# Hybrid encoder step: the output projection's and the FFN's first operands are loaded and split inside the stage in front of them, and the first norm's rows and weights come first in the DMA queue

## The reference

```python
def _layer(l, x, ...):
    z = _rms(x, w["norm1_g"]) @ w["w_in"]          # first norm and input projection
    ...                                            # four mixers: A window, B differential, C latent, M memory
    o = jnp.concatenate([oa, ob, oc, om], axis=-1) # each (B, S, 256)
    x = x + o @ w["w_o"]                           # output projection, 1024 x 1024
    y, new["conv"] = _conv_ffn(_rms(x, w["norm2_g"]), prev, w["f_win"], cw, cb, w["f_wout"])
    return x + y, new

def _conv_ffn(h, prev, w_in, cw, cb, w_out):       # D_FF = 2816
    up = jnp.concatenate([prev.astype(h.dtype), h @ w_in], axis=1)
    ...                                            # causal conv of width 3, c = a | b
    return (jax.nn.silu(a) * b) @ w_out, up[:, S:]
```

## Time and profile before

| | |
|---|---|
| median of 3 runs | 3217.75 us (3211.58 to 3218.52) |
| the profiled execution | 3207.85 us, span of its trace 3205.8 us |
| mean granted TensorE clock | 0.941 of full |
| busy: TensorE, VectorE, ScalarE, GpSimd | 2896.8, 1747.3, 1206.6, 125.9 us |
| DMA engines' share of the span | 15.7% |

### The profile page before, as it was taken

The page is one execution under the profiler, slowest core; times in us unless marked ns, Lnnn a source line. Parts: engine busy times, 40 slices in busy tenths (PEclk is TensorE's granted clock), DMA queues, the critical chain, the costliest instruction groups (busy, mean ns, idle before and its releaser), DMA issues. The chain is left out here.

```text
span 3205.8 us, 49139 instructions
## 1 busy us (share of the span) xinstructions
PE 2896.8 (90%) x19104; PEld 2739.9 (85%) x19104; DVE 1747.3 (55%) x2837; ACT 1206.6 (38%) x2561; POOL 125.9 (4%) x248
## 2 busy tenths in 40 slices
PE   6888879789899999999978888788789999999997
PEld 5686768579899999999957768667789999999997
DVE  3467754643555555555545596465436555545554
ACT  5556644652322222222246574456423222212223
...
DMA packets 182224, 160.89 MB, mean 50 GB/s; under 512 B 14488, under 2 KB 169880, under 8 KB 181528
## 3 DMA queue, kind: packets, MB, share of 16 engines
q1 hardware_dynamic: 182040, 158.45, 15.7%
...
## 5 line engine op out<-in xcount | busy, mean ns | idle before, releaser
L1837 PE MATMUL ps<-h_hi,w_hi 128*128 128x352 f32 x2496 | 546.6, 327 | 43.3 <-DVE w_lo L1948 22.7
L1837 PE MATMUL ps<-h_hi,w_lo 128*128 128x352 f32 x2496 | 540.1, 324 | 0.0
L1837 PE MATMUL ps<-h_lo,w_hi 128*128 128x352 f32 x2496 | 539.9, 324 | 0.0
L1837 PEld LDWEIGHTS ps<-h_hi,w_hi 128*128 128x128 f32 x2496 | 426.8, 190 | 49.3 <-issue 28.0
L1837 PEld LDWEIGHTS ps<-h_hi,w_lo 128*128 128x128 f32 x2496 | 430.4, 189 | 0.0
L1837 PEld LDWEIGHTS ps<-h_lo,w_hi 128*128 128x128 f32 x2496 | 426.6, 189 | 0.0
L2288 ACT ACTIVATE cv<-up,cols 128x1058 f32<-128x1058 f32 x88 | 112.1, 1273 | 718.8 <-issue 678.8
L770 PE MATMUL ps<-w_hi,h_hi 128*128 128x256 f32 (+1 forms) x1088 | 317.3, 292 | 21.6 <-DVE w_lo L998 19.8
L771 PE MATMUL ps<-w_lo,h_hi 128*128 128x256 f32 (+1 forms) x1088 | 311.9, 287 | 0.0
L772 PE MATMUL ps<-w_hi,h_lo 128*128 128x256 f32 (+1 forms) x1088 | 310.2, 285 | 0.0
L2399 DVE TENSOR_TENSOR x_t<-ps,x_t 128x1056 f32<-128x1056 f32 x176 | 221.0, 1256 | 161.0 <-PE ps L1837 160.3
(11 more groups left out here) (227 smaller groups left out, 4280.7 us busy)
## 6 DMA issues: line engine op xcount, KB each, us to landing
...
```

Of the source, the lines that this page charges most:

```text
L1837: last = pe.matmul(ps[:, s0 + b, 0:BAND], lh, rh_[:, b * BAND:(b + 1) * BAND], start=(first_k and n == 0), stop=(last_k and n == 2))
```

## The change

1. `FirstNorm`: the gain of the first norm is loaded a second time, by itself, as the first DMA (`gain_rows`); the four parts of the weights follow at once, and the five row loads come behind them. TensorE turns the 8 gain rows by themselves behind the means; `high` and `low` take `gain_cols`. The transpose of all 112 rows is moved behind TensorE's first products, ahead of the transposes of mem, and ScalarE's copy of it behind its eighth `high`.
2. Attention C gets `prepare`: at its start SyncE loads the four feature blocks into the places of their own `h_lo` blocks and the weights m = 0, 1 into `h_lo` blocks 3 and 2. In jobs 12, 16, 20 and 24 ScalarE writes one `h_hi` block (behind the next job's exponent) and VectorE the `h_lo` block in place.
3. `w_o_block` has no `o_in`. ScalarE and VectorE begin with the splits of m = 0, 1 from `w_raw`. SyncE begins with the frames of C, then of B, then weights m = 2, 3, then `x_t`.
4. In `w_o_block`, behind m = 7 of the weights, the first two units of `f_win` are loaded into `stage` and split in iteration m = 6 of ScalarE and VectorE into weight buffers 2 and 0. `ffn_block` takes over the three buffers, and the count of splits starts at two.

The core of the diff:

```diff
@@ FirstNorm.sync
+            sp.dma_start(self.gain_rows[:, :], I["norm1_g"][layer].rearrange("(c p) -> c p", p=P)).then_inc(S.gain_loaded, 16)
+            weights(sp)
             sp.dma_start(rows[2 * c2:2 * c2 + 8, 0, :], I["norm1_g"][layer].rearrange("(c p) -> c p", p=P)).then_inc(S.par_loaded, 16)
...
-            weights(sp)
@@ FirstNorm.tensor, tensor_mem
-            self.columns(pe, 0)
+            pe.wait_ge(S.gain_loaded, 16)
+            pe.transpose(ps[:, 7, 0:8], self.gain_rows[:, :], ident[0:8, 0:8]).then_inc(S.gain_turned, 1)
...
             if n == 0:
+                self.columns(pe, 0)
@@ attention_stage, vector and scalar
+                    if prepare and j >= 12 and (j - 12) % 4 == 0 and (j - 12) // 4 < 4:
+                        prepare.low(dve, (j - 12) // 4)
...
+                    if prepare and j >= 12 and (j - 12) % 4 == 0 and (j - 12) // 4 < 4:
+                        prepare.high(act, (j - 12) // 4)
@@ new class OutPreparation
+        def sync(self, sp):
+            for i, k in enumerate(OUT_BY_FEATURE):
+                sp.dma_start(self.raw[i], o_dram[k * P:(k + 1) * P, :]).then_inc(self.sems[i], 16)
+            wv = I["w_o"][self.layer].rearrange("(k p) n -> p k n", p=P)
+            for m in range(2):
+                sp.dma_start(self.w_raw[m], wv[:, :, m * P:(m + 1) * P]).then_inc(S.w_loaded0, 16)
+        def high(self, act, i):
+            act.wait_ge(self.sems[i], 16)
+            act.copy(h_hi[:, OUT_BY_FEATURE[i], :], self.raw[i]).then_inc(S.pre_high, 1)
+        def low(self, dve, i):
+            dve.wait_ge(S.pre_high, i + 1)
+            dve.tensor_tensor(h_lo[:, OUT_BY_FEATURE[i], :], self.raw[i], h_hi[:, OUT_BY_FEATURE[i], :].bitcast(F32),
+                              ALU.subtract).then_inc(S.pre_low, 1)
@@ w_o_block, sync
-                load_feature(0)
-                load_w(0)
-                load_feature(1)
-                load_w(1)
-                load_feature(2)
+                load_tokens(256, S.small_loaded)
                 load_tokens(0, S.out3)
-                load_feature(3)
-                load_tokens(256, S.small_loaded)
+                load_w(2)
+                load_w(3)
                 sp.dma_start(x_t[:, :, :].rearrange("p k t -> p (k t)"), x_spill).then_inc(S.out0, 16)
-                for m in range(2, KC):
+                for m in range(4, KC):
                     load_w(m)
+                win = I["f_win"][layer].rearrange("(k p) (s m c) -> s m p k c", p=P, s=2, c=P)
+                for j in range(2):
+                    sp.wait_ge(S.act_lo, KC - 1 + j)
+                    sp.dma_start(stage[:, j, :, :], win[j, 0]).then_inc(f_sem[j], 16)
@@ w_o_block, scalar
+                    if m == KC - 2:
+                        for j in range(2):
+                            act.wait_ge(f_sem[j], 16)
+                            act.copy(w_hi[:, 2 - 2 * j, :, :], stage[:, j, :, :]).then_inc(S.act_hi, 1)
@@ ffn_block, tensor and scalar
-                pe.wait_ge(S.lo_done, 2)
...
                 high_x(0)
-                split(0, 0)
-                split(0, 1)
                 high_x(1)
```

129 lines of the change are left out of this document (70 added, 59 removed).

## The result

| | us |
|---|---|
| changed kernel, 5 executions | median 3183.15 (3177.66 to 3190.42) |
| ratio to the kernel before | 0.9878, 95% interval 0.9838 to 0.9917 |
| forecast | 3191 (3181 to 3203), ratio 0.9917 |
| its profiled execution | 3183.15, span 3181.2, granted clock 0.944 |
| that of before | 3207.85, span 3205.8, granted clock 0.941 |

Faster, as forecast, but by more. Part of the first ratio is luck: it compares means, and the five executions of before that stood beside it, one of them at 3247.70 us, have a mean of 3223.9. The 86 executions of before beside the experiments (one at 3262.61 us with a clock of 0.918, a slow one, is left out) have a mean of 3217.4, standard error 1.1.

What follows compares the result with a forecast made beforehand. TensorE was taken to bound the kernel, busy 2896.8 of 3205.8 us. Terms 11.6 + 1.4 + 10.9 + 2.6 + 1.2 - 1.2 = 26.5 us, off the median 3217.75, gave 3191 us, range 3181 to 3203.

Steps and rivals of the forecast that it cites:

- net 1.2: First norm, both layers: gain of 0.8 + 1.65 us from earlier weights, less 0.6 us a layer for the moved transpose.
- The 1.65 us of layer 1: First norm, layer 1: ScalarE's first split could start about 1619.15 instead of 1620.80, a gain of 1.65 us.
- Output projection, 11.6: Start of the output projection: weights split first, without waiting for o_in; 11.6 us won in both layers, bounds 1.5 to 11.7.
- Just TensorE's own 5.8: Output projection, layer 0: B's norm frees VectorE 5.7 us sooner, matching the 5.8 us won on TensorE's side.
- The term of 1.4 us for m = 2: Output projection: weights m = 2 loaded ahead of x_t save some 0.7 us a layer, 1.4 us; bounds 0 and 2.1.
- FFN, 10.9 and 2.6: FFN start: 10.9 us from earlier f_win splits, 2.6 us from less half-clock work, the latter bounded 0 and 2.6.
- 0.50 for 1 to 2 us only: Sign expected at the FFN's start: its first products run at clock 0.50 for only 1 to 2 us.
- Attention C, -1.2: Attention C: added splits delay job 20's scores and others, 1.2 us lost in both layers; bounds 0 and 18.7.
- the starts moved: Rival, both starts: they don't move because TensorE finds another equal wait behind the barrier; 3216 us, chance 0.06.
- the splits do not stall the stage: Rival, attention C: the splits stall it in full, 18.7 us in place of 1.2; 3209 us, chance 0.06.
- B's frames do not bound: Rival, output projection: B's frames bound it, so the 11.6 us become 1.5; 3201 us, chance 0.10.
- nothing got slower: Rival, attention C: delays from splits are not made up, 38 us lost at a lasting 0.8 us a job; 3229 us, chance 0.04.

Runs made afterwards that it cites:

- again_all: The changed kernel measured once more, nothing edited: 3184.38 us, ratio 0.9889 to the kernel before.
- warm_c_no_norm: The changed kernel without the first norm's part, with two longer unread products ahead of the values of jobs 2 to 11 in attention C: 3187.95 us, ratio 0.9907.
- warm_c: The changed kernel with two longer unread products ahead of the values of jobs 2 to 11 in attention C: 3187.21 us, ratio 0.9899.
- norm_queue: The changed kernel with the first norm's weights loaded behind the five row loads again: 3188.46 us, ratio 0.9912.
- turn_back: The changed kernel with the weights behind the row loads and the transpose of 112 rows ahead of TensorE's first products again: 3186.23 us, ratio 0.9898.
- only_out: The kernel before with only the output projection's part, items 2 and 3 of the change: 3205.13 us, ratio 0.9974.
- b_first: The changed kernel with B's frames asked for ahead of C's: 3184.48 us, ratio 0.9903.
- warm_gaps: The changed kernel with unread products: 14 behind attention C, 7 ahead of the output projection's first product, 24 behind its last weights: 3192.56 us, ratio 0.9926.
- b_first_warm: The changed kernel with B's frames ahead of C's and 14 and 7 unread products around the output projection's start: 3181.07 us, ratio 0.9892.
- m2_late: The changed kernel with the weights m = 2, 3 asked for behind x_t again: 3187.47 us, ratio 0.9899.

## Why the prediction was right, and where it was not

**What the prediction overlooked.** It read attention C as full (89.42 of 90 us busy) and called only the FFN's first 35 us loose. The same row shows a granted clock of 0.91: 17.1 us at half clock, which the sum treats as fixed. It is in this stretch that the traces of one and the same attention C differ most.

**The step that failed** is "It lies 9.9 us under the median of the runs shown, so the median is predicted as 3217.75 - 26.5". It takes for granted that the distance of a profiled execution from the median is the same before and after. Before, the mean of 86 executions lies 9.6 us above the profiled one; after, the mean of 11 lies 1.3 us above it (3184.4 against 3183.15). The clock that the first profile of before had by luck did not come back as a loss in the changed kernel, and 24.7 us between profiles became 33.0 between means. By the long-run mean the changed kernel lies 6.6 us under the forecast of 3191 and inside the range; the other 6 us down to 3178.5 are the five executions of before in the first measurement.

That the profiles agree with the sum to 1.8 us is in part luck too. The output projection and the FFN gave less than their terms (10.0 of 13.0 and 12.1 of 13.5 us); attention C, with other half-speed stretches than in the profile of before, lost 2.4 us net instead of 1.2; and 3.0 us were won in stages that the change does not touch, where again_all has 9.5.

**Where the 8 us come from.** They go with the first norm's part: "net 1.2" is the mis-sized term, 8.1 ± 1.5 alone and 7.3 ± 4.5 when undone. With the longer products in attention C the part is worth nothing that can be told (warm_c_no_norm against warm_c, 0.0 ± 1.7). Its waits are near the forecast: the queue's order is worth 1.3 and 1.0 us (norm_queue against again_all: 0.9 against -0.4, 0.1 against -0.9; forecast 0.8 and 1.65), the late transpose costs 0.3 and 0.8 (turn_back against norm_queue; forecast 0.6 each). The 1.65 us of layer 1 were read from one trace with a long start: from the roots to the first split it took 2.4 us there, and 0.9 to 2.1 in the five other traces without this part. The remainder is spread: of 96 executions of kernels that have the gain rows' own path one lies more than 20 us over the lowest of its kernel, of 135 without it 22 do, with before counted by rounds of measurement. Two of the six traces without it hold an attention C at half clock for 71.7 us, none of the fourteen with it. How a load, a transpose and a copy of eight rows some 560 us earlier do this is not settled. Order and lead in time were tried and do not explain it. The length of the stretch does go with the position of attention C against the clock, but nothing shows how the first norm's part keeps it off the one position with 71.7 us.

**Output projection, 11.6.** The two gaps are 5.1 and 5.5 us shorter, and the waits of 0.49 and 0.46 us behind them are gone, 5.6 and 5.9 in all, as the first step has it. The stages are shorter by 10.0 us (changed), 11.3 (again_all) and 10.7 (only_out), with the 1.4 us for m = 2 within: 2 to 3 us less than 13.0. "Just TensorE's own 5.8" was the right bound, by b_first, but TensorE's own came out smaller: it starts sooner into a half-speed stretch that does not end sooner by as much. In layer 0 it makes products at half clock for 6.06 us; the window of the kernel before has 3.31 (in layer 1 about 5.5 and 4.4):

```profile
698.50:710.30 11.80, 3.31 (x10) 2.88 (x11) 5.25 (x6) 5.31 (x5) 0.00 (x0) 0.50 0.95 306
```

Half of the difference, 1.4 us and in layer 1 some 0.5, is the loss. For the norm of B the prediction writes 8.05 - 1.07 = 7.3 us; the difference is 6.98, and 7.3 comes only with the 0.75 us that its bounds take for the cast. 7.2 us were measured (703.76 to 711.00). B's frames, at 9.65 us instead of 8.8, stand right behind it, as warm_gaps and b_first_warm show. The term of 1.4 us for m = 2 named a wait that went (1.04 and 0.90 us of TensorE's), but by another cause: m2_late lacks it too.

**FFN, 10.9 and 2.6.** The gap went in full. With the clock the stages are 12.1 and 12.2 us shorter against 13.5, so the clock gave 1.3 where 2.6 were forecast: products at half clock 3.2 against 4.8 us and 2.9 against 3.9, half of each difference. "0.50 for 1 to 2 us only" did not come true. The Trainium skill (TensorE: Matmul & The Clock Gate, "What's actually happening") has it that activity releases the throttle. The trace agrees here: before, with the gap behind the means, the stretch ended 13.1 and 12.0 us after their start; without the gap it ends 5.9 and 5.5 us after it. The sum took the stretch to start with the means; in the traces it begins 0.5 to 1.7 us ahead of them, in the idle time at the barrier. In attention C TensorE is busy 68.43 of 71.70 us and the clock stays down, so a busy row is not enough to read the clock from.

**Attention C, -1.2.** 0.5 and 0.6 us, as forecast, at equal stretches. The wait for job 20's scores has no row of its own; only the comparison at equal clock shows it.

**The rivals.** None came true: the starts moved, the splits do not stall the stage, B's frames do not bound, and nothing got slower. All that was left out of the range lay on the slow side, while the surplus came on the fast one.
